# S5 matrices of two thirds made between the memory projections' panels, a second V buffer, and the last third's sums three head steps earlier

## What is computed

```python
ar, ai, bbr, bbi = s5_discretize(lam_re, lam_im, log_dt, b_re, b_im)   # 48 groups, 64 states, 16 channels
bu_r = jnp.einsum('btgc,gpc->btgp', uf, bbr); bu_i = jnp.einsum('btgc,gpc->btgp', uf, bbi)
pr, pim, hr, hi = lax.associative_scan(_ssm_combine, (a_r, a_i, bu_r, bu_i), axis=1)
hr = hr + pr * h0r - pim * h0i
hi = hi + pr * h0i + pim * h0r
y = einsum('btgp,gcp->btgc', hr, c_re) - einsum('btgp,gcp->btgc', hi, c_im)
y = jax.nn.gelu(y.reshape(bsz, t, SEQ_WIDTH) + d_skip * u)
y = y * jax.nn.sigmoid(y @ w_glu + b_glu)
...
mem_out = mem_attention(q_mem, mem_ks[l], mem_vs[l])     # 4 heads over 256 memory tokens
o = concatenate([seq_out, mem_out]) @ p['w_out'][l]
```

## Time and profile before

| | us |
|---|---|
| median of 3 runs (1594.39 to 1602.13) | 1596.81 |
| the profiled execution | 1600.32 |
| span of its first to its last instruction | 1598.5 |
| PE busy | 1436.6 (90%) |
| DVE busy | 978.1 (61%) |
| POOL busy | 670.7 (42%) |
| ACT busy | 616.4 (39%) |

### The profile page before, as it was taken

One profiled execution on the slowest core, in us unless ns is written; L12 is line 12 of the kernel. 1 busy time (PEld: TensorE's weight loads), 2 busy tenths in 40 slices (PEclk: granted clock), 3 DMA queues, 4 the chain that ended last, 5 costly groups with the idle time before them and its releaser, 6 DMA issues.

```text
span 1598.5 us, 32348 instructions
## 1 busy us (share of the span) xinstructions
PE 1436.6 (90%) x12081; PEld 1330.4 (83%) x12081; DVE 978.1 (61%) x1560; ACT 616.4 (39%) x1005; POOL 670.7 (42%) x429
## 2 busy tenths in 40 slices
PE   6985697879998999999798989988889989999996
PEld 6984576879998999999788966556889989999996
DVE  5768917566776046764637678652577771267755
ACT  4552435345563134332414235421355641243312
POOL 0686331333433434443177888301423343344430
PEclk9997758999999999999899999988989999999998
DMA  5433462222333233333145759985213332233321
GB/s 169 123 93 76 73 170 67 78 68 55 94 94 86 77 92 90 92 94 91 40 122 151 223 163 301 327 279 152 83 42 91 91 94 78 79 92 92 99 78 59
DMA packets 288903, 180.43 MB, mean 113 GB/s; under 512 B 54072, under 2 KB 274396, under 8 KB 288748
## 3 DMA queue, kind: packets, MB, share of 16 engines
q1 hardware_dynamic: 288812, 179.20, 38.8%
HBM read 167.10 MB, written 10.63 MB: 111 GB/s over the span
## 4 chain that ended last, share of the span: by engine, by line
PE 55%; DVE 18%; issue 11%; POOL 7%; ACT 4%; DMA 2%; SPq 2%; DVEq 1%; ACTq 0%; POOLq 0%
PE big L2477 43%; ACT yc L2339 3%; PE misc L2561 2%; PE misc L2547 2%; DVE tmp L1193 2%; DVE rstd L1152 1%; DVE hf L1724 1%; POOL s5s L915 1%; PE big L2800 1%; DVE uc L1709 1%; SPq L577 1%; DVE yc L1719 1%; DVE y L1641 1%; POOL e_tmp L915 1%; DVE yc L1716 1%
## 5 line engine op out<-in xcount | busy, mean ns | idle before, releaser
L911 POOL TENSOR_TENSOR w_lo<-raw,w_hi 128x1024 fp32r<-128x1024 f32 (+2 forms) x163 | 423.7, 2600 | 769.1 <-ACT w_hi L2023 768.8
L2477 PE MATMUL big<-x_hi,w_hi 128*128 128x264 f32 x2168 | 452.4, 290 | 40.4 <-DVE x_lo L1183 24.2
L2477 PE MATMUL big<-x_hi,w_lo 128*128 128x264 f32 x2168 | 439.9, 285 | 0.0
L2477 PE MATMUL big<-x_lo,w_hi 128*128 128x264 f32 x2168 | 438.3, 284 | 0.0
L2023 ACT ACTIVATE w_hi<-raw 128x1024 fp32r<-128x1024 f32 (+2 forms) x179 | 198.3, 1108 | 520.0 <-PE big L2477 483.8
L2477 PEld LDWEIGHTS big<-x_hi,w_hi 128*128 128x128 f32 x2168 | 337.7, 190 | 52.1 <-issue 42.5
L2477 PEld LDWEIGHTS big<-x_lo,w_hi 128*128 128x128 f32 x2168 | 336.1, 190 | 0.0
L2477 PEld LDWEIGHTS big<-x_hi,w_lo 128*128 128x128 f32 x2168 | 336.0, 190 | 0.0
L1713 DVE SCALAR_TENSOR_TENSOR yc<-uc,convw,yc 128x512 f32<-128x512 f32 x88 | 106.1, 1206 | 114.3 <-ACT yc L2339 114.3
L2477 PE MATMUL big<-h_hi,w_hi 128*128 128x264 f32 x704 | 144.6, 287 | 15.2 <-DVE h_lo L1728 12.0
L2477 PE MATMUL big<-h_lo,w_hi 128*128 128x264 f32 x704 | 143.0, 285 | 0.0
(11 more groups left out here) (401 smaller groups left out, 2035.8 us busy)
## 6 DMA issues: line engine op xcount, KB each, us to landing
raw<-in_w_up SPq DMA_DIRECT2D x88, 512.0 KB, 3.9
raw<-in_w_down SPq DMA_DIRECT2D x32, 704.0 KB, 4.5
areas<-in_cache_v SPq DMA_DIRECT2D x42, 384.0 KB, 4.7
areas<-in_cache_k SPq DMA_DIRECT2D x41, 384.0 KB, 4.3
raw<-in_w_in SPq DMA_DIRECT2D x16, 512.0 KB, 4.3
raw<-in_w_out SPq DMA_DIRECT2D x16, 512.0 KB, 4.2
raw<-in_w_kv SPq DMA_DIRECT2D x12, 512.0 KB, 4.4
spare<-in_cache_k SPq DMA_DIRECT2D x12, 384.0 KB, 3.9
```

What stands on the lines that cost most here:

```text
L911: pool.tensor_tensor(w_lo[slot][:, 0:kb, :], raw[slot][:, 0:kb, :], w_hi[slot][:, 0:kb, :].bitcast(F32), ALU.subtract).then_inc(lo_made, 1)
L2477: ins = pe.matmul(big[2 * slot + b_][:, 0:c1 - c0], w[slot][:, k, :], r[:, c0:c1], start=(k == 0 and n_ == 0), stop=(k == kb - 1 and n_ == 2))
```

## The change

1. The loop of DVE over the memory panels gets five pieces, one behind each of panels 2 to 6: `s5_b(1)` (the input matrix of third 1), the two halves of `bp` of third 1, the two halves of `cp` of third 0. Behind the loop DVE makes `cp` of third 1, ahead of states(0).
2. States(0) is then followed by `bp` of third 2 alone, states(1) by `cp` of third 2 alone. POOL makes only `bb` of third 2.
3. There are two `v` and two `bp`; `bb[1]`, `v[1]`, `bp[1]` and `u[1]` get other addresses, so that POOL's zeroing of `u[1]` waits for the last memory panel.
4. SP issues `bc_load(1)` ahead of the stores of z, and `bc_load(2)` right behind `u_load(1)`. In the last third it issues the `toep` DMAs ahead of `y_store(1)`.
5. PE does `c_turn(1)` behind bT(0), and ACT `c_copy(1)` ahead of V(0)'s copies; `make_decay` stands ahead of `mem_turned(7)`.
6. `y_sums(2)` and `read_y(2)` move from step 4 of the memory heads to step 1. gelu(0) and gelu(1) move to step 7, ahead of that step's `copy_turned`.

```diff
-                if t + 1 < THIRDS:
-                    sp.wait_ge(s_("b_used"), t + 1)
-                    sp.wait_ge(s_("cT_made"), t + 1)
-                    bc_load(t + 1)
                 if t:
                     full(sp, ("Y", t - 1, 3))
                     if t + 1 < THIRDS:
                         u_load(t + 1)
-                    y_store(t - 1)
+                        y_store(t - 1)
...
+                if t + 1 == THIRDS:
+                    y_store(t - 1)
                 if t:
                     y_return(t - 1)
...
+                if i == 2:
+                    s5_b(1)
+                elif i == 3:
+                    s5_product(1, bp[1], (0,), CHUNK, bb[1])
+                elif i == 4:
+                    s5_product(1, bp[1], (1,), CHUNK, bb[1])
+                    mark(s_("bp_ready"))
+                elif i == 5:
+                    dve.wait_ge(s_("cT_made"), 1)
+                    s5_product(0, cp[0], (0,), CHUNK + 1, cT)
+                elif i == 6:
+                    s5_product(0, cp[0], (1,), CHUNK + 1, cT)
+                    mark(s_("cp_ready"))
+            dve.wait_ge(s_("cT_made"), 2)
+            s5_product(1, cp[1], (0, 1), CHUNK + 1, cT)
...
-                if t + 1 < THIRDS:
-                    dve.wait_ge(s_("b_used"), t + 2)
-                    full(dve, ("bT", t, 3))
-                    s5_product(t + 1, bp, (0, 1), CHUNK, bb[(t + 1) % 2])
+                if t == 0:
+                    dve.wait_ge(s_("b_used"), 3)
+                    s5_product(2, bp[0], (0, 1), CHUNK, bb[0])
                     mark(s_("bp_ready"))
...
+                elif t == 1:
+                    dve.wait_ge(s_("cT_made"), 3)
+                    full(dve, ("Y", 0, 3))
+                    s5_product(2, cp[0], (0, 1), CHUNK + 1, cT)
...
             for n in range(STEPS[0]):
+                if n == Y_AT:
+                    y_sums(THIRDS - 1)
                 if n == SPLIT:
-                    y_sums(THIRDS - 1)
                     fin_turns()
```

More of the change, by code:

```diff
@@ L119, in misc_jobs @@
     for t in range(THIRDS):
-        jobs += [*[("bT", t, a) for a in range(TP // 2)], *[("V", t, a) for a in range((TP + 2) // 3)]]
-        jobs += [("Y", t - 1, a) for a in range(TG // 4) if t]
-        jobs += [("K", t, a) for a in range(TG // 4)] + [("cT", t + 1)] * (t + 1 < THIRDS)
+        jobs += [("bT", t, a) for a in range(TP // 2)] + [("cT", 1)] * (t == 0)
+        jobs += [("V", t, a) for a in range((TP + 2) // 3)] + [("Y", t - 1, a) for a in range(TG // 4) if t]
+        jobs += [("K", t, a) for a in range(TG // 4)] + [("cT", 2)] * (t == 1)
     jobs += [("Y", THIRDS - 1, a) for a in range(TG // 4)]
@@ L174 @@
 SPLIT = 4
+Y_AT, GELU_AT = 1, 7
 MK = 6
@@ L659, in _ @@
             ys3 = y_dram.rearrange("(g c) n -> c g n", c=CH)
+            sp.wait_ge(s_("b_used"), 1)
+            sp.wait_ge(s_("cT_made"), 1)
+            bc_load(1)
             sp.wait_ge(s_("z_ready"), KS)
@@ L679, in _ @@
             u_load(1)
+            sp.wait_ge(s_("b_used"), 2)
+            sp.wait_ge(s_("cT_made"), 2)
+            bc_load(2)
             for l in range(2):
@@ L1260, in s5_factor, with s5_b @@
                 tt(sl(FI), sl(FI), sl(T0), ALU.mult)
-            def s5_b():
-                dve.wait_ge(s_("bc_in"), 16 * 6)
+            def s5_b(t):
+                js = slice(t * TP, t * TP + TP)
+                dve.wait_ge(s_("bc_in"), 16 * 6 * (t + 1))
                 tv = tmp[0][:, 0:TP * CH].rearrange("p (j c) -> p j c", c=CH)
-                f_r, f_i = (sl(n)[:, 0:TP].unsqueeze(2).to_broadcast([P, TP, CH]) for n in (FR, FI))
-                cmul(bb[0][:, 0], bb[0][:, 1], f_r, f_i, b_in[:, 0], b_in[:, 1], tv)
+                f_r, f_i = (sl(n)[:, js].unsqueeze(2).to_broadcast([P, TP, CH]) for n in (FR, FI))
+                cmul(bb[t][:, 0], bb[t][:, 1], f_r, f_i, b_in[:, 0], b_in[:, 1], tv)
                 mark(s_("b_used"))
@@ L1298, in beside_win0 @@
                     s5_factor()
-                    s5_b()
+                    s5_b(0)
                 elif m == 4:
                     dve.wait_ge(s_("powers_ready"), 1)
-                    s5_product(0, bp, (0,), CHUNK, bb[0])
+                    s5_product(0, bp[0], (0,), CHUNK, bb[0])
                 elif m == 5:
                     reciprocal_mem()
-                    s5_product(0, bp, (1,), CHUNK, bb[0])
+                    s5_product(0, bp[0], (1,), CHUNK, bb[0])
                     mark(s_("bp_ready"))
@@ L2213, in gelu @@
                 sync()
+            make_decay()
+            mem_turned(7)
             for t in range(THIRDS):
@@ L2222, in _ @@
                 if t == 0:
[L2223 to L2226, removed]
+                    act.wait_ge(s_("cp_ready"), 1)
+                    c_copy(1)
+                elif t == 2:
+                    act.wait_ge(s_("hp_ready"), 1)
+                    act.wait_ge(s_("hfin_made"), 1)
                 for a_ in range((TP + 2) // 3):
@@ L2230, in _ @@
                     src = bank(("V", t, a_))[:, 0:n * 2 * (NCH + NB)].rearrange("p (j r k) -> p j r k", r=2, k=NCH + NB)
-                    do(A.activation(v[:, 0, 3 * a_:3 * a_ + n], src[:, :, 0, :], ACT.Copy))
-                    freed(own, A.activation(v[:, 1, 3 * a_:3 * a_ + n], src[:, :, 1, :], ACT.Copy), ("V", t, a_))
+                    do(A.activation(v[t % 2][:, 0, 3 * a_:3 * a_ + n], src[:, :, 0, :], ACT.Copy))
+                    freed(own, A.activation(v[t % 2][:, 1, 3 * a_:3 * a_ + n], src[:, :, 1, :], ACT.Copy), ("V", t, a_))
                 mark(s_("v_ready"))
-                if t >= 2:
-                    gelu(t - 2)
                 if t:
@@ L2243, in _ @@
                     mark(s_("kern_ready"))
-                if t + 1 < THIRDS:
-                    c_copy(t + 1)
+                if t == 1:
+                    act.wait_ge(s_("cp_ready"), 2)
+                    c_copy(2)
             kb, n_, base, _ = PH["glu"]
@@ L2249, in _ @@
             for n in range(STEPS[0]):
+                if n == Y_AT:
+                    read_y(THIRDS - 1)
+                elif n == GELU_AT:
+                    gelu(0)
+                    gelu(1)
                 if n == SPLIT:
-                    read_y(THIRDS - 1)
                     hi(kb, base)
@@ L2267, in _ @@
             for t in range(THIRDS):
-                if t:
+                if t == 2:
                     gelu(t)
@@ L2688, in _ @@
                     for n in range(4):
-                        ins = turn(o[:, n * P:n * P + P], bp[:, n % 2, 2 * a_ + n // 2, :], P)
+                        ins = turn(o[:, n * P:n * P + P], bp[t % 2][:, n % 2, 2 * a_ + n // 2, :], P)
                     give(ins, job)
+                if t == 0:
+                    c_turn(1)
                 pe.wait_ge(s_(f"u_in{t % 2}"), 16 * 10 * (t // 2 + 1))
```

39 lines of the change are left out of this document (18 added, 21 removed).

## The result

| | us | ratio to the kernel before |
|---|---|---|
| before, median (in the comparison) | 1599.12 | |
| after, median of 6 (1606.66 to 1612.02) | 1607.32 | 1.0062 [1.0037, 1.0087] |
| after once more, median of 12 (1604.40 to 1611.93) | 1606.15 | 1.0062 [1.0040, 1.0083] |
| after, the profiled execution | 1610.48 | |

The ratio is taken over the single executions of both kernels, with its 95% interval; the quotient of the two medians would be 1.0051.

A forecast was written before the change was run, and what follows sets the result against it. DVE was taken as the bound from 115 to 199 us, with PE waiting. Its 3 us gain was lost through SP: +1.5 and +1.4 for small edits gave 1603.3 profiled, 1600 as median; range 1587 to 1609.

The forecast's parts named there:

- Work moved between the panels: DVE's panel loop: 19.1 us moved into 11.4 of gaps, so the last result comes at 126 instead of 114.68.
- The contention with POOL: DVE's panel loop: 12 operations become new neighbours of POOL's table operations, at 0.3 us each 3.6 us.
- The new wait: DVE ahead of `cp` of third 1, waiting for its `cT`: 5 to 7 us, `cp` beginning at about 133.
- DVE's chain: DVE from `cp` of third 1 through states(2): ends at 195.5 instead of 198.3, a gain of 3 us.
- The chain through SP: Y(0), then SP's loads, stores and `toep`: Y(0) low from 153.5, Y(1) at 183.4 against 184.3 before.
- Then 6.7 and 3.6, as before: PE's Y(1) and K(2) keep their earlier times of 6.7 and 3.6 us, so K(2) ends at 193.7.
- rival (a): Y(1), K(2), first scores run at PE's low clock after a wait near 4 us: 1607 us, chance 0.29.
- The evidence against (a): Ahead of Y(1): bT(2)'s transposes come just ahead, as before, when Y(1) ran at clock 0.97.
- The sums at step 1: Memory heads: `y_sums(2)` waits for `toep` until 204.9, ending sums and steps at 228.2 against 226.7 before.
- The gelus: Step 7 of the heads: gelu(0) and gelu(1) ahead of the copy delay PE's sums and DVE's reciprocal by 1.4 us.
- Rival (c): Heads' steps and sums stay at the high clock as the wait ahead of step 0 shrinks: 1589.5 us, chance 0.12.
- Such light matmuls never brought the clock up in the rows: Heads' steps: the argument against their running at the high clock, which would make the kernel faster.

The follow-up runs named there:

- the moved matrices alone: Changed kernel with the last third's sums back at step 4 and the gelus in their old places: 1596.30 us, ratio 0.9998 to the kernel before.
- `cT` early: Changed kernel with sums at step 4, gelus in old places, third 1's `cT` turned ahead of `mem_turn(1, 3)`: 1591.98 us, ratio 0.9957.
- the last run: Changed kernel, sums at step 4, gelus in old places, `cT` early, 13, 12, 8 idle multiplications ahead of Y(0), Y(1), step 0: 1581.56 us, ratio 0.9902.

## Why the forecast was wrong, step by step

- **Work moved between the panels.** I had the last result at 126 (122.4 to 129); it was read at 127.76. The contention with POOL was right in sum: `s5_b(1)` took 3.12 us of operations instead of 1.74 (two at 0.92 and 1.04, four at 0.29), `bp` 9.60 instead of 7.47, together 3.5 more where I had 3.6. The prediction read its rows as a loss of 0.31 of POOL's 0.62 us, less than a full block. This trace shows that each engine waits for all that is left of the other's operation. DVE's operations end their own length less 0.14 to 0.17 us behind POOL's: 98.36 behind 98.21 (0.29 alone), 107.34 behind 106.26 (1.25 alone), 189.64 behind 189.09 (0.69 alone). A long operation loses only 0.3 to 0.4 us of POOL's 0.62, since a little overlaps on either side (POOL's operation ends 0.48 us behind DVE's, not 0.61). That agrees with the exclusion that the Trainium skill states (SBUF, "Who interferes with whom"). The rows of these pairs that do not stand above:

```profile
97.31 0.90 POOL L922 TENSOR_TENSOR e_tmp<-s5s,e_r 128x384 f32<-128x384 f32 x1
...
104.78 1.48 POOL L922 TENSOR_TENSOR e_tmp<-s5s,e_r 128x256 f32<-128x256 f32 x1
105.82 1.52 DVE L1200 TENSOR_TENSOR tmp<-pw_i,bb 128x1024 f32<-128x1024 f32 x1
...
186.66 2.43 POOL L1026 TENSOR_TENSOR y<-y,yz 128x1040 f32<-128x1040 f32 x1 [1.23 <-DMA yz<-y_scratch]
```

- **The new wait.** 5 to 7 us with `cp` of third 1 at 133; measured 5.79 and 133.97. Right.
- **DVE's chain.** `hp_ready` of third 0 at 153.5, states(2) ends at 195.5; measured 154.8 and 197.5. The collision with `add_z` came, in states(2) (2.77 instead of 0.69).
- **The chain through SP.** Y(0) at the low clock: right, 10.9. Y(1) at 183.4; measured 185.44, 1.5 us of it from Y(0)'s later start.
- **"Then 6.7 and 3.6, as before": this is the step that failed.** Y(1) came behind a wait of 5.81 us, longer than the 4 us that I had named as the point from which rival (a) decides, and ran low: 10.95 instead of 6.7 (+4.3). K(2) took 5.1 instead of 3.6 (+1.5). With the 2.0 us of the later start K(2) ended at 201.5 and not at 193.7. The experiment with 20 and 12 idle multiplications shows that the wait does this: with PE kept busy Y(1) takes 6.55 and K(2) 3.7, and the wait at step 1 is gone. The evidence against (a), that the transposes of bT(2) come just ahead "as before", left out what stands between: before, Y(1) followed V(2) without a wait. In the kernel with the moved matrices alone V(2) took 2.22 us, its high-clock time, and Y(1) still ran low behind a wait of 8.83 us.
- **The sums at step 1.** A wait on `toep` until 204.9, and `fin_turns` at 228.2; measured 212.24 and 235.47. Both are 7.3 late, almost wholly the 7.8 of K(2)'s end. That the wait cannot hide at step 1 was right.
- **The gelus.** 1.4; measured 2.4.
- **What I had not counted.** From `fin_turns` to `glu` the kernel before took 27.3 us, most of it at the low clock up to 239.8; the changed one 25.2 with the gelus in it, since the clock had come up by then. That gave back 4.5, against the 2.4 of the gelus. In sum: 1.5 forecast up to `fin_turns`, 7.3 more there, 2.1 less behind it with the gelus counted in, which gives 6.7 of the 6.6 measured.
- **Rival (a)** had the right mechanism and nearly the right number, 7.2 us in other shares: the scores, for which it had 2.0, ran high (1.99 us for eight), K(2) lost 1.5 and not 2.8, and Y(1)'s late start stood in their place. That its 1607 meets the median so closely is in part luck: in the trace it would have put `glu` 10.1 us later than before, and 6.6 were measured. **Rival (c)**, the heads at the high clock, had the right price: 10.5, where steps and sums measured 9.9 us shorter with the wait filled. It is probably what a third of the executions of the kernel before do; none of these was profiled, so this is not shown. In the changed kernel as it stands no execution was that fast. I had read one profiled execution as if it were the kernel. "Such light matmuls never brought the clock up in the rows" was true of the rows, and did not carry over: with the moved matrices alone the clock came up in `y_sums(2)`.

## What to carry to other kernels

When work is taken off the engine that bounds a stage, ask which engine waits there now and what clock it will come back with: a wait on PE can be paid twice, once as the wait and once in what follows. Where PE alternates between waits and short bursts, a few idle multiplications into a free bank, fewer than the wait holds, can pay for themselves: here 8 of them gave the kernel before 0.41%, while the moved matrices gave nothing alone and 0.43% with `cT` early. And an order that exposes a DMA wait can lose more than the wait: the sums at step 1 cost 7.0 us in the traces, with a wait of 4.72, though `toep` was issued no later (202.18 with the sums at step 1, 202.63 with them at step 4).

## What the runs showed of the hardware

- The same steps of the heads run at 0.50 for as long as 39 us with PE busy for 38.74 of them, or at 1.00 from the start, and which one it is goes with what stood ahead of them. In the changed kernel the clock fell behind a wait of only 1.87 us after the two score banks: the first scores of step 0 took 1.16 us for four, the transposes right behind them 1.11 instead of 0.66. The length of the wait alone does not decide: in the last run K(2) took 3.67 us, its high-clock time, behind a wait of 2.04. The Trainium skill (TensorE: Matmul & The Clock Gate, "HAM oscillation — how this bites in real kernels") says that idle gaps of PE lower its clock and the work behind them is paid at the low one; the runs with the waits filled agree.
- The two groups of times of one and the same kernel, 8.7 us apart in their medians, go with the granted clock over the span (0.948 and above, or below), and filling one wait of 3.8 us put most executions (8 of 12) at or below the times of the faster one.
- An idle 128x256 multiplication in float32 took 0.44 us at the high clock.
- A DVE operation with two inputs in SBUF and one of POOL exclude each other until the first ends: of POOL's 128x1040 addition DVE waited out the rest, and its 128x512 operation took 2.77 instead of 0.69 us.
